# ScalarE reads gates before it cuts the slot's weight, and issues the second weight's load itself

## The chip, the cores and the metric
One core of one Trainium2 chip runs the whole program. The metric is the device time of that core in microseconds. Its engines are TensorE (PE, with its weight loads listed apart as PEld), VectorE (DVE), ScalarE (ACT), GpSimd (POOL) and SyncE (SP), each with an instruction stream of its own. The streams meet only through semaphores. Loads and stores are issued by SP, ACT and POOL.

## What is computed
Two layers over 1024 tokens of width 2048. Each layer is one wide input projection, two mixers side by side (attention over chunks of 64 tokens, and a gated linear recurrence), and an output projection that is added to the residual:

```python
for l in range(2):
    h = _rmsnorm(x, norm_gain[l])
    proj = einsum('bsd,de->bse', h, w_in[l])          # 2048 -> 4352
    q, k, v, g_attn, x_rnn, g_rnn = split(proj)
    attn = _swa_sink_attention(q, k, v, sinks[l], cos, sin)
    xc = _causal_conv(x_rnn, conv_w[l], conv_b[l])
    rnn = _rg_lru(xc, w_rgate, b_rgate, w_igate, b_igate, lru_param)
    mixed = concat([attn * silu(g_attn), rnn * silu(g_rnn)])
    x = x + einsum('bse,ed->bsd', mixed, w_out[l])    # 2048 -> 2048
return _rmsnorm(x, final_gain)
```

In `_rg_lru` the two gates are `r = sigmoid(xc @ w_r + b_r)` and `i = sigmoid(xc @ w_i + b_i)`, with small block-diagonal weights. The step that the change moves on ScalarE is the reading of these two gates out of PSUM.

## The kernel before
The tokens are done in two halves of 512 (`h` = 0, 1), each half through two layers (`l` = 0, 1). Each half-layer is 200 slots: 17 groups of the input projection and 8 of the output projection, 8 slots each. A group yields two tiles of 128 features by 512 tokens. In the first half a slot is mostly one unit: a weight block of 256 KB (128 x 512 float32), used by 12 matmuls of 512 columns. In the second half, groups 7 to 15 of the input projection and the output groups use seven products in place of eight, and a slot may hold half-width units (12 matmuls of 256 columns), two of them, or none; part of their weights comes back ready-made from memory (`READY`).

Products are made in three passes of a high and a low part. So each weight goes through a chain:

- SP loads it into a ring of six buffers (`w_load`, line 517), when the unit six before it is done.
- ACT rounds it to the high part (`weight_hi`, line 947), three units ahead of TensorE (`AHEAD` = 3).
- DVE subtracts to get the low part (`weight_lo`, line 1349), after the high part.
- PE waits for the low part (`w_lo`) and multiplies (line 724 for whole units, 745 for half-width units).

All other work is put by hand into the slots of the same streams, and each engine goes through its slot in a fixed order. On ACT a slot begins with `weight_hi` of the first unit three ahead, then the high parts of summed weights and operands, `attn_out`, then `gate_out`, and later the rest. On DVE a slot begins with sums and residuals, then `weight_lo`, and nearly at its end comes `conv` (lines 1601 to 1604). Each `weight_lo` and `weight_hi` is waited for before the stream goes on.

The recurrence of tile `j` (0 to 7) starts at slot `R0[j]` = 48, 56, 64, 72, 88, 96, 104, 112. The steps that matter here:

- PE does the two small gate products at the ends of slots `R0[j] + 5` (part 0) and `R0[j] + 7` (part 1), line 872. Both write the same PSUM bank `ps_g`, so part 1 waits for `i_done` of part 0.
- ACT does `gate_out`, which waits for that product (`g_done`) and then does two tanh reads (lines 1144 and 1146), at slots `R0[j] + 6` and `R0[j] + 8`.
- DVE's `softmax_max` is in slots 38, 46, ..., 94. It comes after `weight_lo` and ahead of `conv`.
- DVE's `conv` takes an `x_rnn` tile out of its PSUM bank (line 1602) and counts `evac` up. Tiles 1, 3, 5 and 7 are taken in slots 54, 70, 94 and 110 in the first half (`XR_EV`), and two slots after the group's end in the second.
- PSUM has two pairs of banks for the projection. `next_bank` makes PE wait, before the last matmul of a group, for `evac` to show that the pair of the next group is empty. In the first half that is the end of slots 55, 71, 95 and 111 for those tiles.

At the start, SP issues x tile 0, weights 0 and 1, x tile 1, weight 2 and so on (lines 519 to 522). ACT issues the gains (line 1167). PE runs 9 warm-up matmuls (line 679) until the first weight and operand are there, and then `first_units` (line 791) for units 0 and 1.

Of the kernel before, what the change touches and what calls it, by code (L numbers as in the profile page):

```python
# [24 lines left out]
RT = 8  # L25
# [80 lines left out]
def key_of(l, kind, g, j):  # L106

    what = {"lead": LEAD, "late": LATE_OF}[kind][j][0] if kind in ("lead", "late") else None
    if kind == "plain":
        return ("plain", l, g, j)  # L110
    if kind == "block":
        return ("block", l, g, j)
    return ("block", l, g, WHOLE[what]) if what in WHOLE else ("sum", l, g, SUMS[what])
# [3 lines left out]
for at in ((h, l, s) for h in range(HALVES) for l in range(DEPTH) for s in range(SLOTS)):  # L117
    h, l, s = at
# [63 lines left out]
def stores_through(n):  # L182

    return sum(m % RING == n % RING for m in STORED if m <= n)
# [10 lines left out]
def slot_of(what, t):  # L195

    return STREAM.index((GROUPS.index((what, t // 2)), UPG - 1)) + 1
# [18 lines left out]
R0 = [slot_of("xr", j) + 8 * (j % 2) for j in range(RT)]  # L216
# [29 lines left out]
def build(nc, xt, w, blocks, gates, par, fgain, cossin, ident, out):  # L246
    with ExitStack() as ctx:
# [3 lines left out]
        def over(name, at, shape, dt=F32R):  # L251
            return nc.alloc_sbuf_tensor_at(name, [P, *shape], dt, offset=at)

        def sem(name):
            return ctx.enter_context(nc.semaphore(name))
# [9 lines left out]
        wall = over("wall", nc.sbuf_base - 4 * RING * 2 * KU * GW, [RING, 2, KU * GW], F32)  # L265
# [62 lines left out]
        w_in = [sem(f"w_in{i}") for i in range(RING)]  # L328
# [124 lines left out]
        def source(n):  # L453

            h, l, kind, g, j = UNIT[n]
            if kind == "plain":
                return w[l, g, j]
            if kind == "block":
                return blocks[j, l, g].rearrange("r (q c) -> (r q) c", c=TOK)
            what = (LEAD if kind == "lead" else LATE_OF)[j][0]  # L460
            if what in WHOLE:
                return blocks[WHOLE[what], l, g].rearrange("r (q c) -> (r q) c", c=TOK)
            return sums[SUMS[what], l, g].rearrange("r (q c) -> (r q) c", c=TOK)

        def batch_of(l, g):

            return next(n for n, (bl, first, size) in enumerate(BATCH) if bl == l and g - first in range(size))
# [4 lines left out]
        def per_layer(h, l, count, n):  # L472

            return h * (DEPTH * count) + (l * count + n)
# [15 lines left out]
        def x_sem(k):  # L490

            return x_in[KT // 2] if k == 1 else x_in[k // 2]

        @block.sync
        def _(sp_):
# [8 lines left out]
            def w_load(n):  # L504

                at = n if n < TOTAL else n - UPG
                h, l, kind, g, j = UNIT[at]
                what = {"lead": LEAD, "late": LATE_OF}[kind][j][0] if kind in ("lead", "late") else None
                if what in SUMS:
                    sp_.wait_ge(built[what], 32 * (batch_of(l, g) + 1))  # L510
                if n in READY:
                    from_n = CUT_AT[key_of(l, kind, g, j)]
                    sp_.wait_ge(cut_out[from_n % RING], 16 * stores_through(from_n))
                    sp_.dma_start(wcut[:, n % RING, :, :].rearrange("p a c -> p (a c)").bitcast(F32),
                                  cuts[KEYS.index(key_of(l, kind, g, j))]).then_inc(w_in[n % RING], 16)
                    return
                sp_.dma_start(wall[:, n % RING, 1, :], source(at)).then_inc(w_in[n % RING], 16)

            sp_.dma_start(mixed[:, 0, :], xt[0, :, 0, :]).then_inc(x_sem(0), 16)
            w_load(0)  # L520
            w_load(1)
            sp_.dma_start(mixed[:, 1, :], xt[0, :, 1, :]).then_inc(x_sem(1), 16)
            w_load(2)
            x_load(0, 1)
# [7 lines left out]
            for h in range(HALVES):  # L532
                for l in range(DEPTH):
                    for s in range(SLOTS):
# [47 lines left out]
                        if s + 8 in R0:  # L582
                            j = R0.index(s + 8)
# [357 lines left out]
        def _(act):  # L941
            def weight_hi(u):

                act.wait_ge(w_in[u % RING], 16 * (u // RING + 1))
                if u == 1:
                    act.wait_ge(w_hi, 1)
                act.activation(wcut[:, u % RING, 0, :], wall[:, u % RING, 1, :], ACT.Copy).then_inc(w_hi, 1)  # L947
# [161 lines left out]
            def attn_out(h, l, p):  # L1109

                kv, c = 2 * p // NCH, 2 * p % NCH
                act.wait_ge(v_done, per_layer(h, l, NP, p + 1))
                if l == 0 and p == 0 and (h, l, "in") in ZONES:
                    act.wait_ge(xsum_done, at_t(h, l, "in", NPAIR - 1))
                for i in range(2):
                    for odd in range(2):
                        t0 = CH * (c + i)
                        act.activation(mixed[HD * odd:HD * odd + HD, TPK * kv:TPK * kv + TPK, t0:t0 + CH],  # L1118
                                       ps_v[HD * i:HD * i + HD, :, odd, :], ACT.Copy).then_inc(attn_done, 1)
# [16 lines left out]
            def gate_out(h, l, j, part):  # L1136

                act.wait_ge(g_done, per_layer(h, l, 2 * RT, 2 * j + part + 1) + 2 * GRING)
                if j > 0 and part == 0:
                    act.wait_ge(m2_done, per_layer(h, l, RT, j))  # L1140
                if j > 1 and part == 0:
                    act.wait_ge(scan_done, per_layer(h, l, RT, j - 1))
                a, b = HD * part, HD * (1 - part)
                act.activation(r_in[a:a + HD, :], ps_at[a:a + HD, 3, :], ACT.Tanh, scale=0.5,  # L1144
                               bias=pars[a:a + HD, l, C_BR + j:C_BR + j + 1]).then_inc(r_done, 1)
                act.activation(i_in[j % 2][a:a + HD, :], ps_at[b:b + HD, 3, :], ACT.Tanh, scale=0.5,
                               bias=pars[b:b + HD, l, C_BI + j:C_BI + j + 1]).then_inc(i_done, 1)
# [17 lines left out]
                act.activation(mu[:, :], mu[:, :], ACT.Sqrt, scale=0.0625).then_inc(mult_done, 1)  # L1165

            act.dma_start(pars[:, 0, 0:C_SINK], par[:, 0, 0:C_SINK]).then_inc(gain_in, 16)
            act.wait_ge(dve_set, 1)
            act.activation(eps[:, 1:2], eps[:, 0:1], ACT.Copy)
            act.wait_ge(gain_in, 16)  # L1170
# [18 lines left out]
            for h in range(HALVES):  # L1189
                for l in range(DEPTH):  # L1190
                    for s in range(SLOTS):
                        for u in BEAT[h, l, s][:1]:
                            if u > 0 and u + AHEAD < TOTAL and u + AHEAD not in READY:
                                weight_hi(u + AHEAD)

                                act.wait_ge(w_hi, SPLIT_NO[u + AHEAD])
# [8 lines left out]
                        for p in range(NP):  # L1205
                            if s == VAL[p] + 1:
                                attn_out(h, l, p)
                        for j in range(RT):
                            if s in (R0[j] + 6, R0[j] + 8):
                                gate_out(h, l, j, (s - R0[j] - 6) // 2)  # L1210
                        if h == 0 and l == 0 and s == R0[0]:

                            act.wait_ge(dve_set, 4)
# [718 lines left out]
```

## Time and profile before

| | us |
|---|---|
| median of 3 runs | 2282.32 (2281.32 to 2282.64) |
| profiled execution | 2282.06 |
| its span on the core | 2280.3 |
| outside the span | 1.8 |
| PE busy | 2272.6 (100%) |
| PEld busy | 1944.7 (85%) |
| DVE busy | 1579.9 (69%) |
| ACT busy | 1323.6 (58%) |
| POOL busy | 95.1 (4%) |

The ends of matmuls are modelled, so they overlap, and a PE that reads 100% busy may still start its next matmul late. What TensorE loses is read from the distance between starts, and from the idle time of the weight loads. Times in the views are counted from the start of the span.

### The profile page before, as it was taken

How to read it: one execution, taken by the hardware profiler on the slowest of the kernel's cores; microseconds unless marked ns; L12 is line 12 of the kernel's file. 1: busy time of each engine (PE TensorE's matmuls, PEld its weight loads, DVE VectorE, ACT ScalarE, POOL GpSimd, SP SyncE). 2: the span in 40 equal slices, each digit the busy share in tenths (PEclk: the TensorE clock that was granted, in tenths of full speed). 3: DMA queues.
4: the chain of work that ended last, by engine and by line, in shares of the span. 5: the costliest groups of instructions: out<-in, count | busy, mean ns of one | idle time of the engine just before them, and what ended most of it. 6: DMA issues, size and time to landing. Idle time of an engine off the chain costs nothing.

```text
span 2280.3 us, 38665 instructions
## 1 busy us (share of the span) xinstructions
PE 2272.6 (100%) x14590; PEld 1944.7 (85%) x14590; DVE 1579.9 (69%) x2622; ACT 1323.6 (58%) x2556; POOL 95.1 (4%) x154
## 2 busy tenths in 40 slices
PE   9999999999999999999999999999999999999998
PEld 8888888899888888889988888888988888888998
DVE  7658768656556876865677777786568468778555
ACT  7558676445445867645665575664455557566444
POOL 1210000000120000000010000000001200000000
PEclk9999999999999999999999999999999999999999
DMA  8887777544787777765475566676547856666544
GB/s 271 242 216 247 236 240 241 168 139 137 216 223 197 232 238 239 248 173 166 138 226 172 152 199 200 216 233 189 144 130 251 239 172 194 212 199 194 155 133 153
DMA packets 177946, 454.39 MB, mean 199 GB/s; under 512 B 21472, under 2 KB 25824, under 8 KB 172512
## 3 DMA queue, kind: packets, MB, share of 16 engines
q1 hardware_dynamic: 169776, 384.71, 53.1%
q0 software_dynamic: 7552, 67.12, 12.4%
q8 instruction: 115, 1.88, 0.3%
q14 instruction: 71, 0.58, 0.1%
q10 hardware_dynamic: 432, 0.10, 0.0%
HBM read 373.19 MB, written 145.75 MB: 228 GB/s over the span
## 4 chain that ended last, share of the span: by engine, by line
PE 98%; DMA 1%; ACT 0%; DVE 0%; issue 0%; POOL 0%; DVEq 0%; ACTq 0%; POOLq 0%
PE proj L724 73%; PE proj L745 20%; PE ps_at L853 2%; PE ps_at L828 1%; PE ps_at L872 1%; DMA wall<-in_w 1%; PE proj L764 1%; DMA wall<-weight_sums 0%; PE proj L791 0%; PE ps_at L679 0%; DVE mixed L1835 0%; ACT L1144 0%; ACT gy L1053 0%; PE ps_at L806 0%; ACT wcut L947 0%
## 5 line engine op out<-in xcount | busy, mean ns | idle before, releaser
L724 PE MATMUL proj<-operand,wcut 128*128 128x512 f32 x7320 | 1703.3, 391 | 0.1
L724 PEld LDWEIGHTS proj<-operand,wcut 128*128 128x128 f32 x7320 | 1363.6, 188 | 289.3 <-issue 8.8
L1349 DVE TENSOR_TENSOR wcut<-wall,wcut 128x512 fp32r<-128x512 f32 x811 | 558.5, 689 | 536.3 <-ACT wcut L947 530.0
L947 ACT ACTIVATE wcut<-wall 128x512 fp32r<-128x512 f32 x810 | 509.2, 629 | 574.6 <-DMA wall<-in_w 280.7
L745 PEld LDWEIGHTS proj<-operand,wcut 128*128 128x128 f32 x1620 | 206.2, 191 | 7.1
L745 PE MATMUL proj<-operand,wcut 128*128 128x256 f32 x1620 | 208.3, 283 | 0.0
L745 PE MATMUL proj<-xsum_out,wcut 128*128 128x256 f32 x1296 | 160.5, 283 | 0.0
L745 PEld LDWEIGHTS proj<-xsum_out,wcut 128*128 128x128 f32 x1296 | 158.2, 192 | 0.6
L745 PE MATMUL proj<-xsum_in,wcut 128*128 128x256 f32 x864 | 111.8, 284 | 0.0
L745 PEld LDWEIGHTS proj<-xsum_in,wcut 128*128 128x128 f32 x864 | 107.9, 191 | 3.5 <-issue 1.7
L1053 ACT ACTIVATE gy<-proj 32x512 f32<-32x512 f32 x144 | 85.0, 590 | 15.6 <-PE proj L724 9.8
L1105 ACT ACTIVATE prob<-ps_at,stat 128x128 f32<-128x128 f32 x256 | 90.2, 367 | 0.7
L1144 ACT ACTIVATE sqr<-ps_at,pars 64x512 f32<-64x512 f32 x64 | 43.8, 685 | 62.5 <-PE ps_at L872 62.1
L636 POOL DMA_DIRECT2D weight_sums<-in_blocks x36 | 18.2, 512 | 1350.2 <-PE proj L724 1349.8
L1118 ACT ACTIVATE mixed<-ps_at 64x256 f32<-64x256 f32 x128 | 48.6, 380 | 43.2 <-PE ps_at L853 39.2
L1010 ACT ACTIVATE sqr<-x 128x512 f32<-128x512 f32 x62 | 36.8, 635 | 49.8 <-DVE x L1661 49.8
L642 POOL DMA_DIRECT2D weight_sums<-in_blocks x72 | 57.5, 847 | 192.6 <-DMA weight_sums<-weight_sums 104.0
L1661 DVE TENSOR_TENSOR x<-proj,x 128x512 f32<-128x512 f32 x62 | 39.9, 687 | 30.8 <-PE proj L724 30.7
L1446 DVE TENSOR_TENSOR acc<-acc,sqr 128x512 f32<-128x512 f32 x80 | 55.3, 691 | 4.9 <-ACT sqr L1010 0.2
L1105 ACT ACTIVATION_READ_ACCUMULATOR prob<-ps_at,stat 128x1 f32 x256 | 52.7, 206 | 0.0
L1614 DVE SCALAR_TENSOR_TENSOR xc<-xr,pars,xc 128x512 f32<-128x512 f32 x64 | 47.9, 749 | 1.4
L1093 ACT ACTIVATE gt<-gy 128x512 f32<-128x512 f32 x56 | 35.5, 634 | 21.7 <-DVE gy L1551 11.6
(186 smaller groups left out, 1749.0 us busy)
## 6 DMA issues: line engine op xcount, KB each, us to landing
wall<-in_w SPq DMA_DIRECT2D x478, 256.0 KB, 3.0
weight_cuts<-wcut SPq DMA_DIRECT2D x126, 512.0 KB, 3.9
wcut<-weight_cuts SPq DMA_DIRECT2D x126, 512.0 KB, 4.1
wall<-weight_sums SPq DMA_DIRECT2D x180, 256.0 KB, 2.7
weight_sums<-in_blocks POOLq DMA_DIRECT2D x84, 512.0 KB, 6.2
wall<-in_blocks SPq DMA_DIRECT2D x153, 256.0 KB, 2.8
weight_sums<-weight_sums POOLq DMA_DIRECT2D x28, 512.0 KB, 4.4
x<-in_xt SPq DMA_DIRECT2D x16, 512.0 KB, 4.8
```

Source lines behind the costliest of these rows:

```text
L642: pool.dma_start(sums[SUMS[to], l, g:g + size].rearrange("g r e -> (g r) e"), blocks[WHOLE[what], l, g:g + size].rearrange("g r e -> (g r) ...
L724: last = pe.matmul(bank_of(l, 2 * g + m)[:, :], wcut[:, n % RING, a, c:c + P], operand[:, k, b, :], start=(i == 0 and k == 0), stop=(k == ...
L745: last = pe.matmul(bank_of(l, 2 * g + m)[:, HT * half:HT * half + HT], wcut[:, n % RING, a, P * i:P * i + P], src, start=(kind == "lead" a ...
L853: last = pe.matmul(ps_v[HD * i:HD * i + HD, t, :, :], vkey[kv][rows, 2 * c + b, :], probT[rows, :, i, :, SB * b:SB * b + SB], start=b == 0 ...
L947: act.activation(wcut[:, u % RING, 0, :], wall[:, u % RING, 1, :], ACT.Copy).then_inc(w_hi, 1)
L1053: act.activation(gy[dst:dst + 32, 1, :], bank_of(l, tile)[src:src + 32, :], ACT.Copy).then_inc(shift_done, 1)
L1105: act.activation(prob[:, odd, i, pair, :], ps_s[:, odd, i, pair, :], ACT.Exp, scale=HD ** -0.5, bias=stat[:, 1, odd, i, pair:pair + 1], ac ...
L1118: act.activation(mixed[HD * odd:HD * odd + HD, TPK * kv:TPK * kv + TPK, t0:t0 + CH], ps_v[HD * i:HD * i + HD, :, odd, :], ACT.Copy).then_i ...
L1144: act.activation(r_in[a:a + HD, :], ps_at[a:a + HD, 3, :], ACT.Tanh, scale=0.5, bias=pars[a:a + HD, l, C_BR + j:C_BR + j + 1]).then_inc(r_ ...
L1349: dve.tensor_tensor(wcut[:, u % RING, 1, :], wall[:, u % RING, 1, :], wcut[:, u % RING, 0, :].bitcast(F32), ALU.subtract).then_inc(w_lo, 1)
L1446: ins = dve.tensor_tensor(acc[:, :], acc[:, :], sqr[:, k % 2, :], ALU.add)
L1614: mark(dve.scalar_tensor_tensor(xc[:, :], src, wc, xc[:, :], ALU.mult, ALU.add))
```

## The change
On ACT, the two `gate_out` slots are moved from behind `weight_hi`, `lead_copy_out`, `xsum_cut_hi` and `attn_out` to the very front of the slot, in every half and layer: 16 slots in each of four half-layers, 64 calls with 128 tanh reads. DVE, PE and POOL are unchanged. At the start, the load of weight 1 leaves SP's stream, where it was third, and is issued by ACT's queue after the gains. It goes into the same buffer and counts the same semaphore.

```diff
@@ block.sync @@
             w_load(0)
-            w_load(1)
             sp_.dma_start(mixed[:, 1, :], xt[0, :, 1, :]).then_inc(x_sem(1), 16)
@@ block.scalar @@
             act.dma_start(pars[:, 0, 0:C_SINK], par[:, 0, 0:C_SINK]).then_inc(gain_in, 16)
+            act.dma_start(wall[:, 1, 1, :], source(1)).then_inc(w_in[1], 16)
             act.wait_ge(dve_set, 1)
...
                     for s in range(SLOTS):
+                        for j in range(RT):
+                            if s in (R0[j] + 6, R0[j] + 8):
+                                gate_out(h, l, j, (s - R0[j] - 6) // 2)
                         for u in BEAT[h, l, s][:1]:
                             if u > 0 and u + AHEAD < TOTAL and u + AHEAD not in READY:
                                 weight_hi(u + AHEAD)
...
                         for p in range(NP):
                             if s == VAL[p] + 1:
                                 attn_out(h, l, p)
-                        for j in range(RT):
-                            if s in (R0[j] + 6, R0[j] + 8):
-                                gate_out(h, l, j, (s - R0[j] - 6) // 2)
```

## Rows read from the trace of the kernel before
**Rows 1.** The page, section 4: the chain that ended last, by engine.
```profile
PE 98%; DMA 1%; ACT 0%; DVE 0%; issue 0%; POOL 0%; DVEq 0%; ACTq 0%; POOLq 0%
```
**Rows 2.** Waits, whole run: waiter <- waited for: us in total, times, longest.
```profile
ACT sqr L1144 <- PE ps_at L872: 62.1, 36, 4.2
...
PEld ps_at L872 <- ACT vfeat L1146: 1.8, 4, 0.9
...
PEld ps_at L872 <- ACT sqr L1146: 0.6, 1, 0.6
...
PEld proj L724 <- DVE gy L1483: 0.5, 1, 0.5
```
**Rows 3.** Timeline of ACT, slot 70, first half, layer 0: start, duration, instruction, [idle before].
```profile
210.02 1.28 ACT L1144 ACT_TABLE_LOAD   x1 [2.53 <-PE ps_at L872]
...
212.03 0.69 ACT L1146 ACTIVATE sqr<-ps_at,pars 64x512 f32<-64x512 f32 x1
212.74 1.30 ACT L947 ACTIVATE wcut<-wall 128x512 fp32r<-128x512 f32 x2
```
**Rows 4.** Timeline of DVE, slot 70, first half, layer 0.
```profile
210.53 0.68 DVE L1349 TENSOR_TENSOR wcut<-wall,wcut 128x512 fp32r<-128x512 f32 x1
...
213.53 0.68 DVE L1602 TENSOR_TENSOR xr<-proj,rstd 128x512 f32<-128x512 f32 x1
```
**Rows 5.** Timeline of PE, slots 69 to 72, first half, layer 0.
```profile
209.33 0.62 PE L872 MATMUL ps_at<-xcut,gwcut 128*128 128x512 f32 x2
209.79 5.65 PE L724 MATMUL proj<-operand,wcut 128*128 128x512 f32 x24
215.28 0.62 PE L872 MATMUL ps_at<-xcut,gwcut 128*128 128x512 f32 x2
```
**Rows 6.** Timeline of DVE, slot 54, first half, layer 0.
```profile
157.12 1.37 DVE L1349 TENSOR_TENSOR wcut<-wall,wcut 128x512 fp32r<-128x512 f32 x2
...
160.34 0.68 DVE L1602 TENSOR_TENSOR xr<-proj,rstd 128x512 f32<-128x512 f32 x1
```
**Rows 7.** Timeline of ACT, slot 54, first half, layer 0.
```profile
159.18 0.68 ACT L1144 ACTIVATE sqr<-ps_at,pars 64x512 f32<-64x512 f32 x1 [3.91 <-PE ps_at L872]
159.89 0.69 ACT L1146 ACTIVATE sqr<-ps_at,pars 64x512 f32<-64x512 f32 x1
```
**Rows 8.** Timeline of PE, end of slot 55, first half, layer 0.
```profile
164.41 0.62 PE L872 MATMUL ps_at<-xcut,gwcut 128*128 128x512 f32 x2
```
**Rows 9.** Timeline of ACT, slot 118, second half, layer 1.
```profile
2057.04 0.63 ACT L947 ACTIVATE wcut<-wall 128x512 fp32r<-128x512 f32 x1 [4.20 <-DMA wall<-weight_sums]
...
2059.70 0.68 ACT L1146 ACTIVATE vfeat<-ps_at,pars 64x512 f32<-64x512 f32 x1
```
**Rows 10.** Timeline of PE, end of slot 119, second half, layer 1.
```profile
2060.44 0.74 PE L872 MATMUL ps_at<-xcut,gwcut 128*128 128x512 f32 x2 [0.50 <-ACT vfeat L1146]
```
**Rows 11.** Timeline of PE, slots 77 to 80, second half, layer 0.
```profile
1377.18 0.63 PE L872 MATMUL ps_at<-xcut,gwcut 128*128 128x512 f32 x2
...
1382.29 2.91 PE L745 MATMUL proj<-operand,wcut 128*128 128x256 f32 x23
```
**Rows 12.** Timeline of all engines at the start of the program.
```profile
0.99 4.21 PE L679 MATMUL ps_at<-ones 128*128 128x128 f32 x18 [0.99 <-POOL ones L625]
...
1.19 0.90 SPq L517 DMA_DIRECT2D wall<-in_w  x2
...
4.35 0.43 DVE L1687 CAST wcut<-wall 128x512 fp32r<-128x512 f32 x1 [3.02 <-DMA wall<-in_w]
...
4.92 6.49 PE L791 MATMUL proj<-operand,wcut 128*128 128x512 f32 x24
...
5.76 0.63 ACT L947 ACTIVATE wcut<-wall 128x512 fp32r<-128x512 f32 x1 [1.36 <-DMA wall<-in_w]
```
**Rows 13.** Line 791, 4.9 to 6.5 us: duration min/median/max, first and last start.
```profile
L791 PE MATMUL proj<-operand,wcut x4: 497/628/767, 4.9 to 6.3; 128*128 128x512 f32 x4
```
**Rows 14.** Busy time 3 to 5 us: PE PEld DVE ACT POOL, PEclk, DMA share, GB/s.
```profile
3.00:5.00 2.00, 2.00 (x12) 2.00 (x10) 0.65 (x2) 0.72 (x1) 0.00 (x0) 1.00 0.99 326
```

## The prediction
> **What bounds the kernel.** I read the chain of work that ended last first: 98% of it is PE [rows 1], so only what makes PE start a matmul late, or early, can move the end. The busy share can't show that, because ends are modelled. So I read the list of waits next, for the waits of PE and PEld, and then the timelines of ACT, DVE and PE around the moved step. In the list, five gate products of the second half wait for ACT's tanh reads, 1.8 + 0.6 = 2.4 us of idle weight loading, and one unit waits for a PSUM bank, 0.5 us [rows 2]. Nothing else that the change touches reaches PE. So there is little to win, and the question is what the new order makes late.
>
> **Part 1, the gates ahead of the weight, where it gains.** In slot 118 of the last half-layer ACT waits 4.20 us for a weight to land, rounds it until 2057.67, and only then reads the gates, until 2060.38 [rows 9]. PE's second gate product waits for that read and starts at 2060.44 [rows 10]. With the gates in front, this read is no longer behind a DMA. It would start some 0.1 us after its product, as it does where ACT is free, and all five waits of this kind should go. An idle of PEld isn't all lost by PE: a weight load normally stands ready ahead of its matmul. The bank wait tells how much: the start of its matmul comes 0.3 us late and the next one 0.1 us more, so 0.4 of an idle 0.5 us counts. I took 0.15 us off each idle: 2.4 - 5 x 0.15 = 1.6 us. **Gain 1.6 us** (between 1.2 and 2.4, the idle whole).
>
> **Where it costs.** In 36 of the reads of line 1144 ACT stood waiting for PE, 62.1 us in total, with the slot's weight already rounded [rows 2]. There the new order doesn't read the gates sooner, because the product isn't done; it puts the weight behind the wait and behind the read. Slot 70 of the first half shows it. The first gate product starts at 209.33 and ends at 209.95 [rows 5]. ACT had all before it done by 207.49, the slot's weight last, idled 2.53 us, loaded the tanh table from 210.02 and ended its reads at 212.72 [rows 3]. In the new order the reads end at the same 212.72, because the same product releases them. The weight then takes 0.65 us with its gap (two of them took 1.30 [rows 3]), until 213.37, and DVE's low part another 0.04 + 0.68, until 214.09. Before, it ended at 211.21 [rows 4]. So DVE's stream stands 2.88 us longer at `weight_lo`.
>
> The weight itself can wait. PE needs it three units later, which is 8 us in the first half. In the second half some of these are half-width: in slot 78 the first product ends at 1377.81, the low part would be ready 4.14 us later (2.77 to the end of the reads, then 1.37) at 1381.95, and PE wants it after one half-width unit from 1382.29, at some 1383.7 [rows 11]. That leaves 1.8 us, the tightest that I found. SP's store of a rounded weight waits for the low part too. It waits first for the unit before last, 5 us after the product, so it isn't held. No DMA is moved by this part, and POOL waits for neither.
>
> What can't wait is queued behind `weight_lo` on DVE: in slots 54, 70, 94 and 110 of the first half `conv` empties the PSUM tile that PE needs before the last matmul two slots on. In slot 70 `conv` ends 3.00 us after the low part (211.21 to 214.21 [rows 4]), all of it DVE work without a gap. With the low part at 214.09, it ends at 217.09. PE's last matmul of slot 71 is due one spacing ahead of the second gate product: 24 matmuls lie between 209.79 and 215.28, 0.229 us each, so at 215.05 [rows 5]. It would be 2.04 us late. The bank wait of line 1483 is of this same kind, and there the matmul started 0.05 us after the release, and the one behind it 0.11 us later than usual (my reading of the starts around its 0.5 us idle [rows 2]). **Stall at slot 71: 2.04 + 0.16 = 2.2 us.** It comes in both layers: nothing in the arithmetic depends on the layer, as everything counts from the same product.
>
> In slot 54 no table is loaded: reads from 159.18 to 160.58 [rows 7], weight and low part 1.37, so 161.95. `conv` ended 161.02 - 158.49 = 2.53 us after the low part, as the softmax step has no mask here [rows 6]. It would end at 164.48, where PE is due at 164.41 - 0.23 = 164.18 [rows 8]. That is 0.30 + 0.16 = 0.46 us. Slot 94 has the same steps, 0.46. Slot 110 has the table but no softmax step: 2.77 + 1.37 + 0.8 = 4.94 us after its product against 5.10 for the matmul, and its weight load is wanted 0.2 us before that, so only the 0.11 us of the following matmul. Sum for a layer 0.46 + 2.20 + 0.46 + 0.11 = 3.23. **Both layers: 6.5 us lost.** Bounds: if DVE's order hid it, 0; if each of the other 24 gate reads of the first half also cost a late matmul of 0.11 us, 9.
>
> The second half has its `conv` in other slots, with fewer weights of its own to round, and I found no such coincidence there. I take nothing, up to 0.3 us.
>
> **Part 2, the second weight on ACT's queue.** PE starts its first unit at 4.92, released by the cast of weight 0 at 4.35, for which DVE waited 3.02 us on the DMA. Weight 1 is rounded at 5.76 after a DMA wait of 1.36 us on ACT [rows 12]. PE doesn't wait for weight 1 at all, so landing it sooner gains nothing. SP issues both within 0.90 us from 1.19 [rows 12], and without weight 1 the x tile behind it is issued 0.45 us sooner, but at 326 GB/s and a share of 0.99 [rows 14] the DMA engines are full and nothing lands sooner for it. ACT pays 0.4 us of issuing, hidden under its wait for the gains. But the load now goes out beside that of weight 0 instead of behind it. Sharing the engines, the two land together: weight 0 comes later by the time of up to one weight, 256 KB at 326 GB/s = 0.8 us. At the worst it lands with the old weight 1, 1.4 us later. PE then starts at some 5.8. The profile grants the clock at 1.00 there [rows 14], yet the first four matmuls last 497 to 767 ns, as at 1.2 GHz rather than 2.4 [rows 13], and take 1.75 us where four at 0.229 take 0.92. A later start spends less of the slow stretch, if it ends when it did: 0.8 us late costs about 0.5. **Cost 0.5 us** (0 to 0.8, and see the third rival).
>
> The Trainium skill, page "DMA: Bandwidth & Descriptors", section "Issuing engines are not separate DMA queues", says that DMAs of different issuers run on the same engines and interleave, and that more issuers save only the issuer's time. By that rule this part can't gain and weight 0 is delayed; the row with the full DMA share points the same way. If each issuer had engines of its own, the cost would be 0.
>
> **The sum.** 6.5 - 1.6 + 0.5 = 5.4 us more. On the profiled execution, 2282.06, that is 2287.5; that execution lies 0.3 us below the median, well inside the spread of the runs.
>
> **The rivals.**
> First: DVE's delay never reaches PE. DVE is only 69% busy, and a stream with that much slack often absorbs 3 us. For it: in slot 54 the same step has 3.16 us in hand (164.18 - 161.02). Against it: between `weight_lo` and `conv` there is no gap to absorb anything, and slot 70 has 0.84 us in hand (215.05 - 214.21). It decides from a delay under 0.8 us at slot 70; then only the gains and the start remain: 2282.06 - 1.6 + 0.5 = 2281.0, not slower. Chance 0.15.
> Second: only slot 70 stalls, because the small 0.3 us excesses vanish in some earlier start, and the start of the program costs nothing: 4.4 - 1.6 = 2.8, 2284.9. Chance 0.10.
> Third: the pause of PE, now some 0.9 us between the warm-up and the first unit, renews the slow stretch. PE began at 0.99 [rows 12] and was fast from 6.4 [rows 13]; as long again from 5.8 ends at 11.2, and every microsecond in it costs nearly half of one: 2.3 us more, 2289.8. Chance 0.10. The Trainium skill, page "TensorE: Matmul & The Clock Gate", section "What's actually happening", has the clock follow recent activity, which leaves this open; no row here has such a pause.
> Fourth: the new order has no effect, because ACT's stream isn't executed as written. The rows show each engine in the written order, so 0.02, at 2282.
>
> **The numbers.** The forecast has 0.63: 2287.5, from 2286.0 to 2288.8 on its own. 0.2% is 4.6 us, about what a measurement of this kernel can tell from no change, so "slower" begins at 2286.9. The forecast lies close above it: about a quarter of it falls below. Slower: 0.47 + 0.10 = 0.57. Same: 0.16 + 0.15 + 0.10 + 0.02 = 0.43, less 0.03 that I leave for a faster one that I don't see. The range goes from 2283.9 to 2289.8; it leaves out the first rival and the fourth, and a little above.
>
> **What would show it.** Right, if the list of waits has PEld L724 waiting for DVE line 1602: twice some 2.3 us idle and four times about 0.6; if the waits of PEld L872 for lines 1144 and 1146 are gone; if in slot 70 DVE's line 1349 starts right after ACT's line 947, which follows line 1146. Wrong, if line 1602 releases no one, or if DVE still has its weight before the product ends. For the start: the cast of line 1687 later than 4.35, and PE's line 791 after 4.92. The prediction fails most easily at slot 70, as it carries two thirds of the loss.

## The result and the profile after

| | median us (lowest to highest, executions) | its profiled execution, us (span) |
|---|---|---|
| before | 2281.79 (2280.83 to 2282.72, 7) | 2282.06 (2280.3) |
| after | 2288.87 (2286.40 to 2289.93, 7) | 2288.27 (2286.5) |

The changed kernel takes 7.1 us more: 1.0028 times as long, with an interval of 1.0018 to 1.0038. The forecast was 2287.5.

The chain of the kernel after, by engine, answers to [rows 1]. DVE has come into it with 1%:
```profile
PE 97%; DVE 1%; issue 1%; ACT 1%; DMA 0%; SPq 0%; DVEq 0%; ACTq 0%
```
The list of waits of the kernel after (waiter <- waited for: us in total, times, longest) answers to [rows 2]. Lines of ACT and PE have moved up by one, so `gate_out` is at 1143 and 1145 and the gate product at 871:
```profile
DVE wcut L1349 <- ACT wcut L946: 560.8, 346, 6.6
...
ACT sqr L1143 <- PE ps_at L871: 121.2, 48, 5.9
...
PEld proj L723 <- DVE xr L1602: 7.9, 8, 2.4
...
PE proj L723 <- DVE xr L1602: 5.0, 6, 1.9
```
Two things are to be seen. The five waits of the weight loads for the gate reads (1.8 + 0.6 us in [rows 2]) are gone: no line has PEld waiting for ACT's line 1145. And there is a wait that the kernel before didn't have, PE for DVE's line 1602, which is `conv`. ACT's own wait for the product has doubled, 62.1 to 121.2 us, because now it waits there with the weight still to do; that alone costs nothing.

The place of the largest new wait is slot 70 of the first half, layer 0. First ACT in the kernel after (start, duration, instruction, [idle before]), against [rows 3]:
```profile
211.02 1.28 ACT L1143 ACT_TABLE_LOAD   x1 [2.58 <-issue]
212.32 0.69 ACT L1143 ACTIVATE sqr<-ps_at,pars 64x512 f32<-64x512 f32 x1
213.03 0.69 ACT L1145 ACTIVATE sqr<-ps_at,pars 64x512 f32<-64x512 f32 x1
213.74 1.30 ACT L946 ACTIVATE wcut<-wall 128x512 fp32r<-128x512 f32 x2
```
Then DVE in the kernel after, against [rows 4]:
```profile
214.40 0.69 DVE L1349 TENSOR_TENSOR wcut<-wall,wcut 128x512 fp32r<-128x512 f32 x1 [2.18 <-ACT wcut L946]
...
217.41 0.68 DVE L1602 TENSOR_TENSOR xr<-proj,rstd 128x512 f32<-128x512 f32 x1
```
Then PE in the kernel after, against [rows 5]:
```profile
210.33 0.62 PE L871 MATMUL ps_at<-xcut,gwcut 128*128 128x512 f32 x2
210.79 5.41 PE L723 MATMUL proj<-operand,wcut 128*128 128x512 f32 x23
218.15 0.50 PE L723 MATMUL proj<-operand,wcut 128*128 128x512 f32 x1 [1.95 <-DVE xr L1602]
218.49 0.63 PE L871 MATMUL ps_at<-xcut,gwcut 128*128 128x512 f32 x2
```
The order can be read as a relay. The product releases ACT; ACT loads the table and reads the gates until 213.72; only then it rounds the weight; DVE's low part, which in the kernel before had started at 210.53, starts at 214.40; the softmax step and `conv` follow without a gap until 218.09; and the 24th matmul, which needs the tile that `conv` empties, starts at 218.15, where the 23 before it ran in a row. PE stood idle for 1.95 us.

**Where the 6.2 us of the two profiled executions went.** I took the start of each of the 14590 matmuls after, less the start of the same matmul before; a step in that difference is a place where time is lost or won. The times of steps, here and below, are those of the kernel before.

| place | step, us | forecast |
|---|---|---|
| start, until 60 us | +0.02, then +0.35 in small steps | +0.5 |
| first half, layer 0: slots 55, 71, 95 | +0.56, +2.20, +0.53 | +0.46, +2.20, +0.46 |
| slot 111 (both layers) | under 0.06 | +0.11 each |
| 708 us: the bank wait of line 1483 in [rows 2] | -0.43 | none |
| first half, layer 1: slots 55, 71, 95 | +0.54, +3.75, +0.54 | +0.46, +2.20, +0.46 |
| second half, 1370 us: a bank wait of line 1546 | -0.15 | none |
| second half: gate reads (the -0.16 is two of them) | -0.31, -0.16, -0.46, -0.78 | -1.6 together |

The sum is 6.2, as 2288.27 - 2282.06. The step at 708 us is in kernels that leave ACT's order as it was, too (the second experiment), so it belongs to that one execution of before and not to the change. The same holds for the step at 1370 us: in the execution of before the weight load there waited for DVE's line 1546, and eight of the ten other kernels, four of them with the old order in the second half, have the same step of 0.13:
```profile
1369.86 0.19 PEld L724 LDWEIGHTS proj<-operand,wcut 128*128 128x128 f32 x1 [0.28 <-DVE gy L1546]
```
That leaves 1.71 us for the gate reads. One row stands out: slot 71 of layer 1 cost 3.75 instead of 2.20. The stall before it is the same; this is PE there, in the kernel after:
```profile
782.65 5.41 PE L723 MATMUL proj<-operand,wcut 128*128 128x512 f32 x23
790.01 0.50 PE L723 MATMUL proj<-operand,wcut 128*128 128x512 f32 x1 [1.95 <-DVE xr L1602]
```
The difference is behind it. Windows of PE in the kernel after (window, its length, busy time and instructions, granted clock, DMA share, GB/s), first around the stall of layer 1, then around that of layer 0:
```profile
784.00:790.40 6.40, 4.45 (x20) 1.00 0.58 221
790.40:793.80 3.40, 3.40 (x10) 0.51 0.28 77
793.80:797.20 3.40, 3.40 (x17) 0.99 0.26 50
```
```profile
215.00:219.00 4.00, 2.05 (x10) 1.00 0.83 308
219.00:223.00 4.00, 4.00 (x19) 1.00 0.20 68
```
Behind the stall of layer 1 the granted clock is at half, 1.2 GHz instead of 2.4, for 3.4 us, in which PE does 10 instructions where it does 17 in the next 3.4. That costs 3.75 - 2.20 = 1.55 us. PE had been busy again for 0.4 us when the clock fell. Behind the stall of layer 0, with the same idle of 1.95 us, it stays at full. My sum had no term for this.

### The profile page after: what moved, and what is told of

Its sections match the earlier page's. It is cut to its first block, busy times and chain, and to the rows that moved or that the text cites. A ratio compares the mean times of both kernels' runs of the same rounds, so it can differ in the third digit from the quotient of the medians.

```text
span 2286.5 us, 38665 instructions
## 1 busy us (share of the span) xinstructions
PE 2274.5 (99%) x14590; PEld 1944.6 (85%) x14590; DVE 1579.6 (69%) x2622; ACT 1323.0 (58%) x2556; POOL 95.0 (4%) x154
## 4 chain that ended last, share of the span: by engine, by line
PE 97%; DVE 1%; issue 1%; ACT 1%; DMA 0%; SPq 0%; DVEq 0%; ACTq 0%
PE proj L723 72%; PE proj L744 20%; PE ps_at L852 2%; PE ps_at L827 1%; PE ps_at L871 1%; PE proj L763 1%; DVE stat L1573 0%; DMA wall<-in_w 0%; PE proj L790 0%; ACT wcut L946 0%; DVE wcut L1349 0%; ACT sqr L1145 0%; DVE mixed L1835 0%; DVE xr L1602 0%; PE ps_at L805 0%
## 5 line engine op out<-in xcount | busy, mean ns | idle before, releaser
L1143 ACT ACTIVATE sqr<-ps_at,pars 64x512 f32<-64x512 f32 x64 | 43.8, 684 | 121.4 <-PE ps_at L871 121.2
```

## The experiments

My theory: the loss is the stall of PE behind `conv`, most of it in slot 71 of the first half, and the gain is the five gate reads of the second half; the moved weight load costs half a microsecond at the start. The rivals: that the start costs most of it; that it isn't `conv` but the late weights themselves, or the 24 other gate reads; and, once the profile was there, that the fallen clock and not the stall is the loss. All kernels leave the second weight on SP's queue, except the one named.

**The two parts apart.** First the moved gates alone:
```diff
                     for s in range(SLOTS):
+                        for j in range(RT):
+                            if s in (R0[j] + 6, R0[j] + 8):
+                                gate_out(h, l, j, (s - R0[j] - 6) // 2)
...
-                        for j in range(RT):
-                            if s in (R0[j] + 6, R0[j] + 8):
-                                gate_out(h, l, j, (s - R0[j] - 6) // 2)
```


> Part 1 of the change alone: gates ahead of the slot's weight, the second weight stays with SyncE. Theory (the loss is made by DVE's conv coming late behind weight_lo in slots 54, 70, 94 and 110 of the first half): all of the loss is here, 4.9 us above before (6.5 lost, 1.6 gained), plus 1.3 us for each of the two slot-71 stalls at which the granted clock drops. So 4.9 to 7.5 us above before. Rival (the start of the program makes the loss): under 2 us above before.


Measured: 2289.83 (2287.32 to 2290.12, 6) against 2281.74, so +8.1 us, ratio 1.0034 (1.0022 to 1.0046). This is a little above the range that I gave. It is also 1.0 us above the whole change; the two intervals overlap, so no gain of the moved weight load follows from that. Its profiled execution took 2287.32 and has the same steps as the kernel after: 0.55, 2.22, 0.53 in layer 0, 0.55, 2.22, 0.58 in layer 1, the same gains, and one fall of the clock, again behind the stall of layer 1 (window of PE, as above):
```profile
790.00:794.00 4.00, 4.00 (x13) 0.57 0.19 66
```
Here the fall cost 1.57. Stalls less the gains of the gate reads are 6.65 - 1.71 = 4.9 us; with one fall 6.5, with two 8.1. The mean granted clock that is listed for each execution goes with that: it is 0.999 in the two shorter ones (2287.32 and 2288.79) and 0.998 in the four at 2289.82 to 2290.12. The list doesn't say where it fell, so that these four had both falls is an inference, and not a strong one: the mean also holds a stretch at half behind the last matmul, of which 0.5 to 3.7 us lie in the spans of the profiled executions here, and executions of before are listed at 0.999 and at 1.0 alike.

Then the moved weight load alone:
```diff
             w_load(0)
-            w_load(1)
...
             act.dma_start(pars[:, 0, 0:C_SINK], par[:, 0, 0:C_SINK]).then_inc(gain_in, 16)
+            act.dma_start(wall[:, 1, 1, :], source(1)).then_inc(w_in[1], 16)
```


> Part 2 of the change alone: the second weight issued by ACT's queue, gates where they were. Theory: the first unit starts 0.5 us later, and the first three units end within 0.5 us of before; 0 to 0.8 us above before. Rival (a longer slow stretch of TensorE's clock at the start): 2 to 3 us above before in some executions. If the load were free and sooner: 0 or below.


Measured: 2282.19 (2281.39 to 2283.97, 11) against 2281.74, +0.45 us, ratio 1.0002 (0.9993 to 1.0011). By the medians that can't be told from nothing. The start in its timeline shows the mechanism, against [rows 12]:
```profile
1.18 0.42 SPq L517 DMA_DIRECT2D wall<-in_w  x1
1.19 0.45 ACTq L1167 DMA_DIRECT2D wall<-in_w  x1
...
5.21 0.43 DVE L1687 CAST wcut<-wall 128x512 fp32r<-128x512 f32 x1 [3.89 <-DMA wall<-in_w]
...
5.79 1.67 PE L790 MATMUL proj<-operand,wcut 128*128 128x512 f32 x5 [0.58 <-DVE wcut L1687]
```
Both weights are issued at the same time, and the one that PE needs first lands later: its cast starts at 5.21 instead of 4.35, and PE's first unit at 5.79 instead of 4.92. By the second unit 0.39 of these 0.87 us are left: the first unit took 6.00 us instead of 6.49, as the late start spends less of the slow stretch. The Trainium skill, page "DMA: Bandwidth & Descriptors", section "Issuing engines are not separate DMA queues", says that transfers of different issuers run on the same engines and interleave; the cast 0.86 us later agrees with it.

**Half by half.** The gates in front in the second half alone:
```diff
+                            if s in (R0[j] + 6, R0[j] + 8) and h == 1:
...
-                            if s in (R0[j] + 6, R0[j] + 8):
+                            if s in (R0[j] + 6, R0[j] + 8) and not (h == 1):
```


> Gates ahead of the weight in the second half of the tokens only; second weight with SyncE. Theory: the five waits of TensorE for the tanh reads go and nothing takes their place, 1.6 to 1.9 us below before. Rival (the second half also has a late step behind weight_lo): at or above before. Line 1602 should release no idle of PE.


Measured: 2279.83 (2279.27 to 2280.73, 11) against 2281.74, -1.9 us, ratio 0.9992 (0.9983 to 1.0000). In its waits PE and PEld wait neither for the gates nor for `conv`; what DVE still releases on the path is a weight (in this kernel lines of DVE have moved down by three):
```profile
PEld proj L724 <- DVE wcut L1352: 1.2, 4, 0.6
```
The longest of these, 0.6 us, cost 0.5 us at 1560 us in this execution; the kernel after and the first experiment, which have the same order there, don't have that step.

So the gain is real, though the interval just reaches 1.0000: of its eleven executions only one, 2280.73, took longer than the shortest of the 28 of before, 2280.66. And all of the loss is in the first half. What there is to gain differs from one execution to the next. In the seven profiles with the old order in the second half the weight loads wait for the gate reads three to seven times, 1.7 to 4.2 us in total, where the profile of before has 2.4; in the five with the new order they never do. It is the fastest kernel of this study, though 1.9 us is less than 0.2%.

**Which slots of the first half.** The gates in front in slot 70 alone, in both layers:
```diff
+                            if s in (R0[j] + 6, R0[j] + 8) and h == 0 and s == 70:
...
+                            if s in (R0[j] + 6, R0[j] + 8) and not (h == 0 and s == 70):
```


> Gate read ahead of the weight in one slot alone, slot 70 of the first half, in both layers; all else as before. Theory: two stalls of TensorE at the end of slot 71 of 2.2 us each, released by line 1602, and for each of them 0 or about 1.3 us more where the granted clock falls to 0.50 behind it: 4.4 to 7.0 us above before. Rival (the loss is spread over all gate reads): 16 times less than the whole, under 1 us.


Measured: 2288.36 (2285.57 to 2288.84, 6) against 2282.05, +6.3 us, ratio 1.0027 (1.0015 to 1.0038). Two gate reads of 32 in the first half make nearly the whole loss. In its waits the weight loads wait for `conv` twice (here at line 1605):
```profile
PEld proj L724 <- DVE xr L1605: 4.7, 2, 2.4
```
The step of layer 1 is 2.21, that of layer 0 is 3.76: this time the clock fell behind the stall of layer 0, and not behind that of layer 1, as windows of PE in this kernel show:
```profile
217.70:221.10 3.40, 3.40 (x10) 0.50 0.29 84
221.10:224.50 3.40, 3.40 (x16) 1.00 0.25 63
...
788.00:792.00 4.00, 2.64 (x11) 1.00 0.37 118
```
The fall again cost 1.55, and 2.21 + 3.76 are 6.0 of the 6.3 us. (This one execution also has a step of 1.12 at 1370 us, behind a wait of PE for DVE's line 1549. That is the bank wait that the execution of before had there too, with 0.28 us; no run ties its size to the moved read, and I leave it out.) One of the six executions has a mean clock of 1.0, and it is the short one, 2285.57; the others, at 0.998 and 0.999, took 2288.09 or more.

The other slots, without the four that hold a `conv`:
```diff
+                            if s in (R0[j] + 6, R0[j] + 8) and h == 0 and s not in (54, 70, 94, 110):
...
+                            if s in (R0[j] + 6, R0[j] + 8) and not (h == 0 and s not in (54, 70, 94, 110)):
```


> Gate reads ahead of the weight in the first half in all slots but 54, 70, 94 and 110, that is 12 of 16 in each layer; second half as before. DVE's stream is held at weight_lo by 1.4 to 4.5 us in each of them, with nothing behind it that PE needs soon. Theory: within 0.3 us of before. Rival (any delay of weight and DVE costs): 2 us or more above before.


Measured: 2281.63 (2280.00 to 2283.61, 11) against 2282.05, -0.4 us, ratio 1.0000 (0.9991 to 1.0009). In these 24 gate reads the weights are late just the same, and nothing waits for them. PE's waits for ACT are those of the second half, where this kernel keeps the old order:
```profile
PE ps_at L872 <- ACT vfeat L1146: 0.8, 1, 0.8
PE ps_at L872 <- ACT sqr L1146: 0.7, 1, 0.7
```
The weight loads show how much these waits vary; here they are seven, with 4.2 us, where [rows 2] has five with 2.4:
```profile
PEld ps_at L872 <- ACT vfeat L1146: 2.6, 5, 1.3
PEld ps_at L872 <- ACT sqr L1146: 1.6, 2, 1.1
```
In the starts nothing moves in the first half from 60 us on but the step at 708 us. That excludes the late weight, and the 0.11 us for each of these reads that was my upper bound.

**Is it `conv`?** The gates stay in front in both halves, but DVE does `conv` ahead of the low part of the weight:
```diff
+                        if h == 0 and s in XR_EV[h][1::2]:
+                            conv(h, l, XR_EV[h].index(s))
                         for u in BEAT[h, l, s][:1]:
...
                                 weight_lo(u + AHEAD)
...
-                        if s in XR_EV[h]:
+                        if s in XR_EV[h] and not (h == 0 and s in XR_EV[h][1::2]):
                             conv(h, l, XR_EV[h].index(s))
```
`XR_EV[0][1::2]` is slots 54, 70, 94 and 110.


> As the gates alone in both halves, but on DVE the conv of slots 54, 70, 94 and 110 of the first half is put ahead of that slot's weight_lo. Theory: the eight waits for line 1602 vanish, with them all 6.5 us, and the clock doesn't drop; 1.6 to 1.9 us below before. Rival (what is late is DVE or the weights as a whole, not this one step): the loss stays near 5 us, with PE waiting for another line of DVE.


Measured: 2280.18 (2279.27 to 2281.22, 11) against 2281.74, -1.6 us, ratio 0.9992 (0.9984 to 1.0001). With ACT's order exactly as in the first experiment, a swap of two steps on DVE takes away 9.7 us (2289.83 - 2280.18). (Its profiled execution, at 2281.22 the longest of the eleven, has a step of 1.16 us at 147.7 us, at a matmul of line 853 that waited 1.03 us for ACT, that isn't in the others shown here.) DVE in slot 70 of this kernel:
```profile
211.97 0.68 DVE L1602 TENSOR_TENSOR xr<-proj,rstd 128x512 f32<-128x512 f32 x1
...
214.16 0.69 DVE L1349 TENSOR_TENSOR wcut<-wall,wcut 128x512 fp32r<-128x512 f32 x1 [1.30 <-ACT wcut L947]
```
and PE in the same slot, with its 24 matmuls in a row:
```profile
210.54 5.65 PE L724 MATMUL proj<-operand,wcut 128*128 128x512 f32 x24
```
The low part is as late as in the kernel after (214.16; 214.40 there), and it holds no one who is due.

The same swap in slot 70 alone (`h == 0 and s == 70` in both conditions) leaves the small stalls of slots 54 and 94:


> As the gates alone in both halves, with conv put ahead of weight_lo in slot 70 only; slots 54, 94 and 110 stay late. Theory: two stalls of 2.2 us and the clock falls behind them go, two times 1.1 us of stalls stay, 1.9 us are gained: 0 to 0.6 us above before. Rival (slots 54 and 94 carry much of the loss): 3 us or more above before.


Measured: 2282.09 (2281.56 to 2283.57, 11) against 2281.97, +0.1 us, ratio 1.0002 (0.9993 to 1.0010). The steps are 0.55, 0.51, 0.55 and 0.53: 2.1 us lost, less the 1.9 won. PE's wait in this kernel:
```profile
PE proj L724 <- DVE xr L1602: 1.1, 4, 0.3
```
The stalls of 0.3 us idle don't vanish in some earlier start, and none of them is followed by a fall of the clock. (This execution also has a step of 0.82 us at 1179 us, where PE waited for DVE at line 806, and which no other here has.)

**Does the clock fall by the length of the stall?** In the kernel before, with nothing else changed, DVE does idle work ahead of `conv` in slots 70 and 110 of the first half, so that PE stalls four times for a chosen length:
```diff
+                        if h == 0 and (l, s) in N:
+                            mark(dve.memset(lead_v[:, :], 1.0))
+                            for _ in range(N[l, s]):
+                                mark(dve.tensor_scalar(lead_v[:, :], lead_v[:, :], 1.0, None, ALU.mult))
                         if s in XR_EV[h]:
```
`N` gives the number of instructions for layer 0 and 1: 4 and 3 in slot 70 and 11 each in slot 110 for the shortest, three more each for the next, and three more again for the longest. `lead_v` isn't in use there. `mark` makes DVE wait until the instruction is done.


> As before, with idle work put on DVE ahead of conv in slots 70 and 110 of the first half (small in-place products on a buffer that is free there), sized for four PE stalls of about 0.9 us. Measures what a stall of PE costs. Theory: a stall under the size at which the clock falls costs its length and 0.16 us: 4.2 us above before, granted clock 1.00 throughout. Rival (any stall can cost clock): 5.5 us or more above before in most executions.


Measured: 2285.49 (2283.79 to 2287.11, 11) against 2282.05, +3.4 us, ratio 1.0014 (1.0005 to 1.0023). The steps are 1.04, 0.66, 0.98 and 0.69, 3.4 us; the clock stays at full behind all four. (Its execution also has a step of 1.8 us at 1558 us, behind a late weight, and took 0.8 us longer than the median.)


> As the kernel with four stalls, but sized for about 2.1 us each. Theory: 4 x 2.25 = 9.0 us above before, plus about 1.3 us for each stall behind which the granted clock falls to 0.50, in varying number from execution to execution: 10 to 14 us above before and a wider spread than with 0.9 us stalls. Rival (the clock doesn't depend on the stall): 9.0 us above before and the same spread as before.


Measured: 2288.92 (2288.38 to 2289.91, 6) against 2282.05, +6.9 us, ratio 1.0032 (1.0020 to 1.0043). The steps are 2.01, 1.67, 1.94 and 1.65, 7.3 us, and none was followed by a lower clock. I had expected 10 us or more: the stalls came out shorter than I had sized them, and in the profile the falls didn't come. Nor is the spread wider: the six executions lie 1.5 us apart, those of before 3.6.


> As the kernel with four 2.1 us stalls, each three products longer. The shorter ones came out as 2.01, 1.67, 1.94 and 1.65 us with 0.32 us for each product, so these should be 3.0, 2.6, 2.9 and 2.6 us, 11.1 us together. Theory: behind stalls of this length the granted clock falls to 0.50 in nearly every execution, at about 1.3 us each: 14 to 16.5 us above before. Rival (the fall in the changed kernel was not made by the stall): 11.1 us above before.


Measured: 2294.82 (2292.82 to 2297.74, 5) against 2281.97, +12.9 us, ratio 1.0058 (1.0045 to 1.0072). The steps are 3.04, 2.65, 2.96 and 2.70, 11.3 us, and only the third was followed by a fall, which cost 1.56. The median lies between what the theory gave (14 to 16.5 more) and its rival (11.1), and the five executions lie 4.9 us apart, those of before 3.1. PE's waits for `conv` in the kernels with the shortest, the middle and the longest stall:
```profile
PE proj L724 <- DVE xr L1602: 2.4, 4, 0.8
```
```profile
PE proj L724 <- DVE xr L1602: 6.3, 4, 1.8
```
```profile
PE proj L724 <- DVE xr L1602: 10.2, 4, 2.7
```
And windows of PE in the one with the longest, behind its third stall:
```profile
793.20:796.50 3.30, 3.30 (x10) 0.50 0.29 79
796.50:800.00 3.50, 3.50 (x17) 0.99 0.33 108
```
So a stall is paid in full by itself, and a fall of the clock may come on top. In the profiles it came behind three of six stalls with 1.95 us idle (one of two in each of after, the first experiment and slot 70 alone), and behind one of four of 2.4 to 2.7; it came behind none of four of 1.4 to 1.8, and none of four of 0.4 to 0.8. In none of the twelve profiles does it fall anywhere else before the last matmul. So the falls go with the long stalls, but the length alone doesn't decide it. What does is open.

## Why the prediction was right

**The path.** Only PE bounds the kernel, and only late or early matmul starts move its end: the steps of these starts add up to the whole difference of the two executions.

**Slot 70, the main term.** The low part was worked out to end 4.14 us after the product (214.09 for 209.95). It ended at 215.09, for a product that ended at 210.95: 4.14. `conv` ended 3.00 us later, the stall cost 2.20 in layer 0 and as much in layer 1 (with the clock's share taken off), and 2.21 or 2.22 in two other kernels. The forecast was 2.2. The bank wait gave the right size for what a late release costs beyond its own lateness.

**Slots 54 and 94** cost 0.53 to 0.56 instead of 0.46 each. In slot 54 of layer 0 the reads ended at 161.05 and DVE's low part at 162.50, so weight and low part took 1.45 where I had 1.37, and `conv` ended 2.53 us later as forecast; that is most of it. **Slot 110** cost nothing that the starts show, instead of 0.11: in layer 0 the weight load waited 0.16 us for `conv` there, and PE didn't.

**The gain** was 1.9 us by the medians, where 1.6 was forecast, and 1.71 by the starts. Against the profile that it was worked out from it is right: 2.44 us idle in five waits and 1.71 us won is 0.15 us off each, as I took it. The forecast stood on one execution, though, and the idle differs: with 0.15 us off each wait the seven profiles with the old order would give gains of 1.1 to 3.2 us, 1.9 on average. The largest of the five gains is that of slot 118. ACT there in the kernel after, against [rows 9]:
```profile
2059.92 1.28 ACT L1143 ACT_TABLE_LOAD   x1
2062.86 0.68 ACT L1143 ACTIVATE sqr<-ps_at,pars 64x512 f32<-64x512 f32 x1 [1.66 <-PE ps_at L871]
2063.57 0.69 ACT L1145 ACTIVATE vfeat<-ps_at,pars 64x512 f32<-64x512 f32 x1
```
The table is loaded before the product is there, and the reads end at 2064.26, 2.6 us ahead of the second gate product at 2066.85. The wait of [rows 10] is gone, and the starts show 0.78 us won there, more than PE's own idle of 0.50: it is the 0.92 us idle of the weight load there, less 0.14. In slot 70 the same load stands behind the wait, at 211.02, though ACT had been idle for 2.58 us.

**The moved weight load** cost 0.45 us by the medians, which can't be told from nothing, and 0.39 by the starts, where 0.5 was forecast. What is shown is the later cast and the later first unit. In the profiled execution of after it cost only 0.02: there the cast came at 4.84, and the first unit, which began 0.50 later than in [rows 12], took 6.00 us instead of 6.49. By the spacing of PE's matmuls, the slow stretch at the start ends anywhere from 4.4 to 7.0 us in the profiled executions of this study, whatever the kernel. At 60 us the kernels with SP's order stand at -0.60 to +0.39 us against before, so 0.5 us can't be read from one of them.

**The rivals.** The first, that DVE's slack absorbs the delay, fell: slot 70 has 0.84 us in hand and got 2.88. The second, that only slot 70 stalls, fell with the small steps of the last swap, which are all there. The third, that the pause at the start renews the slow stretch, fell: the first unit didn't take longer. The fourth fell with the new order in ACT's rows.

**What the sum lacked.** With the sizes measured, stalls of 6.6, less 1.9, plus 0.45, are 5.2 us, where the forecast had 5.4. The measured 7.1 holds 1.9 us more. The part of it that profiles show is the clock: 1.55 us for a fall, one in the profiled execution. My list of costs of a stall had the wait and the late matmul behind it, and nothing for what PE does after having stood idle. So the forecast was nearly one fall too low. The rest of the 1.9 us is not shown: the waits that change from one execution to the next, by up to 1.8 us in one place, lie in it too. On its own the forecast went up to 2288.8, where the profiled execution (2288.27) is inside and the median of 2288.87 just above. The median lies inside the range only because the range went on to 2289.8 for the third rival, which fell; that this room was there for the missing term is luck.

## What to carry to other kernels

When a step of an in-order engine is moved ahead of another, follow the one that is now late to the next engine, and ask not who needs its result but what is queued behind its consumer there: here the late weight was needed by no one, and the release of a PSUM tile that stood behind it on DVE was due. Look for the single tightest release and not for the mean slack, since a DVE that is 69% busy had 0.84 us in hand at the one place that mattered; put such a release ahead of work that can wait, and the same change wins instead of losing. And move a step only in the stages where the wait exists: the second half alone has the whole gain and none of the loss.

## What the chip showed that I had not expected

- A stall of PE can cost more than its length. After 1.95 us idle in a stretch that was otherwise without a gap, the granted clock was at half for 3.4 us in three of six cases, and each such fall cost 1.55 to 1.57 us in four kernels (after, the first experiment, slot 70 alone, the longest stalls). It began 0.4 to 1.0 us after PE was busy again. Why it comes in one case and not in the next, with the same idle and the same work around it, no run here tells.
- In slot 118 ACT had the tanh table loaded 1.66 us before the wait for the product ended; in slot 70 it loaded it only behind the wait. In the kernel after all twelve table loads of the gate reads in the second half stand ahead of the wait, right behind an instruction of line 963, and all twelve of the first half behind it, each with a `weight_hi` as the instruction before. In the program `weight_hi` is followed by a wait for its own end. No run changes this alone, so that it is the cause is not shown.
- Issued together with another 256 KB load, the first weight landed 0.49 to 0.86 us later, by the start of its cast (4.84 and 5.21 against 4.35; 4.22 to 4.47 in the other kernels with SP's order).
